# Two chained transformer blocks on one core: modulation weights regrouped by feature tile, the first projection woven between the modulation sums

## The reference

```python
silu_c = jax.nn.silu(c)
silu_cc = jax.nn.silu(c_ctx)
mod_l = (silu_c @ ada_w[l] + ada_b[l])[:, None, :]
mod_c = (silu_cc @ ada_w[l] + ada_b[l])[None, None, :]
sh1, sc1, g1, sh2, sc2, g2 = jnp.split(mod_l, 6, axis=-1)
csh1, csc1, cg1, csh2, csc2, cg2 = jnp.split(mod_c, 6, axis=-1)
hl = rms_norm(xl, norm_mix_w[l]) * (1 + sc1) + sh1
hc = rms_norm(xc, norm_mix_w[l]) * (1 + csc1) + csh1
pl = hl @ w_in
pc = hc @ w_in
```

## Time and profile before

| what | value |
|---|---|
| median of 3 runs | 2367.29 us |
| the runs | 2364.22 to 2369.87 us |
| profiled execution, first to last instruction | 2361.5 us (its time outside this span is not recorded) |
| mean granted TensorE clock | 0.983 |
| TensorE busy | 2267.3 us, 96% |
| TensorE weight load busy | 1935.6 us, 82% |
| VectorE, ScalarE, GpSimd busy | 50%, 36%, 40% |

### The profile page before, as it was taken

One profiled execution on the slowest core, in us unless ns is written; L12 is line 12 of the kernel. 1 busy time (PEld: TensorE's weight loads), 2 busy tenths in 40 slices (PEclk: granted clock), 3 DMA queues, 4 the chain that ended last, 5 costly groups with the idle time before them and its releaser, 6 DMA issues.

```text
span 2361.5 us, 37027 instructions
## 1 busy us (share of the span) xinstructions
PE 2267.3 (96%) x14111; PEld 1935.6 (82%) x14111; DVE 1179.9 (50%) x1904; ACT 860.2 (36%) x1411; POOL 939.8 (40%) x770
## 2 busy tenths in 40 slices
PE   6999999999999999999999999999999999999998
PEld 3878889888888888898888878778887887788776
DVE  4785763457777743343143365653333106671273
ACT  5434343241111122335315442223443236543462
POOL 2435442343343433334422255565665440254302
PEclk9999999999999999999999999999999999999998
DMA  7132232135555521112200025553222321122212
GB/s 282 63 144 72 99 126 68 63 125 187 187 186 194 187 99 62 63 62 72 60 14 10 28 92 185 182 193 104 95 92 96 98 89 64 57 81 89 68 46 72
DMA packets 66121, 245.42 MB, mean 104 GB/s; under 512 B 7312, under 2 KB 9616, under 8 KB 65360
## 3 DMA queue, kind: packets, MB, share of 16 engines
q1 hardware_dynamic: 65760, 242.94, 30.0%
q0 software_dynamic: 240, 0.79, 0.1%
HBM read 240.81 MB, written 2.10 MB: 103 GB/s over the span
## 4 chain that ended last, share of the span: by engine, by line
PE 68%; issue 6%; POOL 5%; DVE 4%; ACT 2%; POOLq 0%; DVEq 0%; ACTq 0%
PE ps L862 12%; PE ps L863 11%; PE ps L864 11%; POOL w_low L480 4%; PE ps L1663 4%; PE ps L1665 4%; PE ps L1666 4%; PE ps L1907 2%; PE ps L1894 2%; PE ps L623 2%; PE ps L1880 2%; PE ps L1832 1%; PE ps L899 1%; PE ps L900 1%; PE ps L901 1%
## 5 line engine op out<-in xcount | busy, mean ns | idle before, releaser
L480 POOL TENSOR_TENSOR w_low<-ring,w_high 128x512 fp32r<-128x512 f32 (+2 forms) x534 | 755.8, 1437 | 1126.9 <-ACT w_high L471 1113.9
L471 ACT ACTIVATE w_high<-ring 128x1024 fp32r<-128x1024 f32 (+2 forms) x267 | 274.7, 1031 | 951.4 <-PE ps L864 632.5
L862 PE MATMUL ps<-h_high,w_high 128*128 128x512 f32 x1040 | 412.8, 397 | 17.0 <-POOL h_low L725 7.1
L863 PE MATMUL ps<-h_low,w_high 128*128 128x512 f32 x1040 | 407.6, 392 | 0.0
L864 PE MATMUL ps<-h_high,w_low 128*128 128x512 f32 x1040 | 407.3, 392 | 0.0
L862 PEld LDWEIGHTS ps<-h_high,w_high 128*128 128x128 f32 x1040 | 196.7, 189 | 70.9 <-issue 14.0
L864 PEld LDWEIGHTS ps<-h_high,w_low 128*128 128x128 f32 x1040 | 196.5, 189 | 42.1
L863 PEld LDWEIGHTS ps<-h_low,w_high 128*128 128x128 f32 x1040 | 197.0, 189 | 37.7
L2977 DVE TENSOR_TENSOR hidden<-arena,hidden 128x1536 fp32r<-128x1536 f32 (+1 forms) x42 | 87.2, 2076 | 193.3 <-ACT hidden L2223 193.3
L1663 PE MATMUL ps<-hidden,w_high 128*128 128x512 f32 (+1 forms) x504 | 178.7, 355 | 0.0
L1665 PE MATMUL ps<-hidden,w_high 128*128 128x512 f32 (+1 forms) x504 | 178.6, 354 | 0.0
(11 more groups left out here) (488 smaller groups left out, 4816.1 us busy)
## 6 DMA issues: line engine op xcount, KB each, us to landing
const<-late_w_dram SPq DMA_DIRECT2D x112, 512.0 KB, 4.9
ring<-up_dram SPq DMA_DIRECT2D x88, 512.0 KB, 3.5
ring<-down_dram SPq DMA_DIRECT2D x44, 512.0 KB, 3.4
XB<-ada_dram SPq DMA_DIRECT2D x22, 768.0 KB, 5.4
ring<-winE_dram SPq DMA_DIRECT2D x32, 512.0 KB, 3.6
ring<-win_dram SPq DMA_DIRECT2D x20, 512.0 KB, 3.4
ring<-winC_dram SPq DMA_DIRECT2D x20, 512.0 KB, 3.6
arena<-ada_dram SPq DMA_DIRECT2D x10, 768.0 KB, 18.2
```

What stands on the lines that cost most here:

```text
L471: nc.scalar.activation(WH[p][:, 0:L], RAW[p][:, 0:L], ACT.Copy).then_inc(w_hi, 1)
L480: ins = nc.gpsimd.tensor_tensor(WL[p][:, to], RAW[p][:, to], WH[p][:, to].bitcast(F32), ALU.subtract)
L862: nc.tensor.matmul(bank[:, 0:n], wh[:, cols], hi, start=(k == 0), stop=False)
L863: nc.tensor.matmul(bank[:, 0:n], wh[:, cols], lo, start=False, stop=False)
```

## The change

The modulation weights are regrouped. `FIRST_TILES` lists six groups in which the shift and the scale of a feature tile come together: (8, 0, 9), (1, 10, 2), (11, 3, 12), (4, 13, 5), (14, 6, 15), (7). `first_columns(g)` takes the place of `mod_column` and `gains` for them: on VectorE, one add for each column tile, a wait for them, one small instruction for each gain, a wait again.

The norm's mean follows the first group's sums, the two segments share one mean sum and one root, and the latent spread comes before the second group's sums. Each feature tile of the latent segment is then scaled, shifted and split as soon as its group is there. `first_latent(k)` multiplies latent tile k by both of win0's first two chunks, six matmuls into two PSUM banks, and these calls stand between the sums and the turns of the groups. On ScalarE `shift_high` of the latent tiles is cut into pieces that stand between the calls of `mod_row`. The context segment follows after the latent one.

SP loads win0's chunks 0 and 1 behind the first group's weights instead of behind the last's. The copied rows of the first groups have a place of their own, and the banks of `adaT` and `n0` are changed.

```diff
--- before.py
+++ after.py
@@ -74,7 +74,9 @@
 
 
 
-MODS = [*range(0, 18, 3), *range(16, 46, 3), 45]
+FIRST_TILES = ((8, 0, 9), (1, 10, 2), (11, 3, 12), (4, 13, 5), (14, 6, 15), (7,))
+LATER_MODS = [*range(16, 46, 3), 45]
+MODS = [*FIRST_TILES, *LATER_MODS]
 ADA_COLS = 3 * P
 
 FIRST_MODS = 6
@@ -110,7 +112,7 @@
 )
 
 SUMS = dict(
-    adaT=(FIRST_MODS, (4, 5)), n0=(4, (0, 1, 2, 3)), win0=(19, B5), hgS0=(6 * SCORE_SUMS, (0, 1, 2, 3)), hgK0=(6 + ROUND_MODS[0], (5,)), hgU0=(12, (4, 6)), ro0=(5, (5, 6)),
+    adaT=(FIRST_MODS, (4,)), n0=(3, (1, 5, 6)), win0=(19, B5), hgS0=(6 * SCORE_SUMS, (0, 1, 2, 3)), hgK0=(6 + ROUND_MODS[0], (5,)), hgU0=(12, (4, 6)), ro0=(5, (5, 6)),
     win1=(19, B5), hgS1=(6 * SCORE_SUMS, (0, 1, 2, 3)), hgK1=(6 + ROUND_MODS[1], (5,)), hgU1=(12, (4, 6)), ro1=(5, (5, 6)),
     wmlp=(14, B5), sv=(8, B8), wout0=(16, B8),
     n1=(4, B8), up0=(88, B8), down0=(12, B8),
@@ -158,7 +160,7 @@
 
 PAIRED = (("n2", 0), ("n4", 0))
 
-BATCHED = dict(ro0=(range(4),), ro1=(range(4),), nlat=(range(1), range(1, 5)), nqk=(range(9), range(9, 21)), nB=(range(4),))
+BATCHED = dict(n0=(range(2),), ro0=(range(4),), ro1=(range(4),), nlat=(range(1), range(1, 5)), nqk=(range(9), range(9, 21)), nB=(range(4),))
 RS_COLS = 48
 PARTED = dict(n0=0, n1=2, n2=4, n3=6, n4=7, n5=8)
 
@@ -700,10 +702,10 @@
                 nc.scalar.wait_ge(h_even, KT // 2 * (PARTED[stage] + k) + j // 2 + 1)
                 nc.scalar.activation(dsts[j], dsts[j], ACT.Identity, bias=shifts[j]).then_inc(h_ready, 1)
 
-        def shift_high(stage, k, between=None):
+        def shift_high(stage, k, between=None, some=range(KT)):
 
             _, _, _, dsts, shifts, highs, _ = ITEMS[stage][k]
-            for j in range(KT):
+            for j in some:
                 if between and j == 4:
                     between()
                 await_scaled(nc.scalar, stage, k, j)
@@ -965,6 +967,7 @@
 
         ADA_EARLY, = carve((2 * FIRST_MODS, 4, ADA_COLS))
         ADA_ROW, = carve((3, ADA_COLS), at=ARENA - 3 * ADA_COLS)
+        ADA_ROW_EARLY, = carve((3, ADA_COLS), at=24 * T)
         ADA = [tiles(XB, 4 * ADA_COLS * c, 4, ADA_COLS) for c in range(ADA_SLOTS)]
         at = CONST_AT["masks"][0]
         LATE_W = [const[:, at + x * D:at + (x + 1) * D] for x in range(2)]
@@ -1009,6 +1012,9 @@
 
             return FIRST_MODS + sum(ROUND_MODS[:r]) + n
 
+        def ada_row_at(g):
+            return (ADA_ROW_EARLY if g < FIRST_MODS else ADA_ROW)[:, g % 3, :]
+
         def tiles_of(g):
             return 1 if g == FIRST_MODS - 1 else 3
 
@@ -1299,6 +1305,9 @@
             for u in range(2 * FIRST_MODS):
                 n = tiles_of(u // 2) * P
                 sp.dma_start(ADA_EARLY[:, u, :, 0:n], dram["ada"][u][:, :, 0:n]).then_inc(ada_early[u], 16)
+                if u == 1:
+                    for k in range(2):
+                        load_split(sp, "win0", k, k)
 
             def load_mods(chunks):
 
@@ -1308,8 +1317,6 @@
                         sp.wait_ge(ada_sums if half else ada_half, g + 1)
                     sp.dma_start(ADA[v % ADA_SLOTS], dram["ada"][2 * FIRST_MODS + v]).then_inc(ada_full[v % ADA_SLOTS], 16)
 
-            for k in range(2):
-                load_split(sp, "win0", k, k)
             sp.dma_start(const[:, tables_at:CONST_N], dram["const"][:, tables_at:]).then_inc(tables_in, 16)
             for k in range(2, 4):
                 load_split(sp, "win0", k, k)
@@ -1476,26 +1483,57 @@
                 bank = open_bank(pe, *turn_sums(g))
                 pe.wait_ge(ada_row, g + 1)
                 for i in range(tiles_of(g)):
-                    ins = nc.tensor.matmul(bank[:, 4 * i:4 * i + 4], ADA_ROW[:, g % 3, i * P:(i + 1) * P],
+                    ins = nc.tensor.matmul(bank[:, 4 * i:4 * i + 4], ada_row_at(g)[:, i * P:(i + 1) * P],
                                            C("pick")[:, 0:4], start=True, stop=True)
                 sums_done(ins, *turn_sums(g))
 
             pe.wait_ge(const_in, 32)
             pe.wait_ge(cs_ready, 3)
-            for g in range(FIRST_MODS):
-                mod_sums(g)
-                if g:
-                    mod_turn(g - 1)
-                for k in range(2):
-                    if g == 3:
-                        mean(pe, "n0", k)
-                    if g == 4:
-                        spread(pe, "n0", k)
-            mod_turn(FIRST_MODS - 1)
+
+            def first_latent(k):
+
+                h_there(pe, "n0")(0, k)
+                hi, lo = in_parts(0)(0, k)
+                cols = slice(k * P, (k + 1) * P)
+                for c in range(2):
+                    if k == 0:
+                        await_parts(pe, "win0", c)
+                        open_bank(pe, "win0", 2 * c)
+                    bank, p = bank_ap("win0", 2 * c), split_use("win0", c)[0]
+                    nc.tensor.matmul(bank, WH[p][:, cols], hi, start=(k == 0), stop=False)
+                    nc.tensor.matmul(bank, WH[p][:, cols], lo, start=False, stop=False)
+                    ins = nc.tensor.matmul(bank, WL[p][:, cols], hi, start=False, stop=(k == KT - 1))
+                    if k == KT - 1:
+                        sums_done(ins, "win0", 2 * c)
+
+            mod_sums(0)
+            for k in range(2):
+                mean(pe, "n0", k)
+            mod_turn(0)
+            spread(pe, "n0", 0)
+            mod_sums(1)
+            spread(pe, "n0", 1)
+            mod_turn(1)
+            first_latent(0)
+            mod_sums(2)
+            first_latent(1)
+            mod_turn(2)
+            first_latent(2)
+            mod_sums(3)
+            first_latent(3)
+            mod_turn(3)
+            mod_sums(4)
+            first_latent(4)
+            mod_turn(4)
+            first_latent(5)
+            mod_sums(5)
+            first_latent(6)
+            mod_turn(5)
+            first_latent(7)
 
             def first_chunks(x, stage):
 
-                for s in range(2):
+                for s in range(0 if x else 1, 2):
                     for c in range(2):
                         split_features(pe, stage, c, stage, 2 * c + s, KT, P, in_parts(x), (s,),
                                        ready=None if c else in_there(pe, x) if x else h_there(pe, "n0"))
@@ -2017,23 +2055,27 @@
             def mod_row(g):
                 act.wait_ge(ada_sums, g + 1)
                 cols = tiles_of(g) * P
-                A(ADA_ROW[:, g % 3, 0:cols], ps[:, ADA_BANK, 0:cols], ACT.Copy).then_inc(ada_row, 1)
+                A(ada_row_at(g)[:, 0:cols], ps[:, ADA_BANK, 0:cols], ACT.Copy).then_inc(ada_row, 1)
 
             act.wait_ge(x_in, 32)
             load_table(ROOT)
             for k, j in squared("n0"):
                 square("n0", k, j)
-                if k and j in (2, 4, 6):
-                    mod_row(j // 2 - 1)
-            mod_row(3)
-            for k in range(2):
-                root("n0", k)
-            mod_row(4)
-            mod_row(5)
+            mod_row(0)
+            root("n0", 0)
             for k in range(2):
                 split_hi("win0", k)
-            for k in range(2):
-                shift_high("n0", k)
+            mod_row(1)
+            shift_high("n0", 0, None, (0,))
+            mod_row(2)
+            shift_high("n0", 0, None, (1, 2))
+            mod_row(3)
+            shift_high("n0", 0, None, (3,))
+            mod_row(4)
+            shift_high("n0", 0, None, (4, 5))
+            mod_row(5)
+            shift_high("n0", 0, None, (6, 7))
+            shift_high("n0", 1)
 
             def y_high(y, to, n):
                 for k in range(KT):
@@ -2647,6 +2689,22 @@
             step.link(TT(small[:, 5:6], small[:, 4:5], small[:, 3:4], ALU.subtract))
             step.link(TS(small[:, 5:6], small[:, 5:6], -LAM_INIT, None, ALU.add))
 
+            def first_columns(g):
+
+                turned = await_sums(dve, *turn_sums(g))
+                for i, k in enumerate(FIRST_TILES[g]):
+                    ins = TT(mod[:, 0, k, :], turned[:, 4 * i:4 * i + 2], V("ab0", k).to_broadcast([P, 2]), ALU.add)
+                    if i < tiles_of(g) - 1:
+                        step.mark(ins)
+                taken(ins, *turn_sums(g))
+                step.settle()
+                await_taken(dve, *turn_sums(g))
+                for k in FIRST_TILES[g]:
+                    if k >= KT:
+                        step.mark(STT(gain[:, 0, k - KT, :], mod[:, 0, k, :], 1.0, V("nm0", k - KT).to_broadcast([P, 2]),
+                                      ALU.add, ALU.mult))
+                step.settle()
+
             def mod_column(g):
                 k, n = MODS[g], tiles_of(g)
                 turned = await_sums(dve, *turn_sums(g))[:, 0:4 * n].rearrange("p (i v) -> p i v", v=4)
@@ -2686,17 +2744,26 @@
             for k, j in squared("n0"):
                 if j:
                     add_square("n0", k, j)
-                if k and j in (4, 6):
-                    mod_column(j // 2 - 2)
-            for k in range(2):
-                invert("n0", k)
```

(33 more changed lines are left out.)

## The result

The kernel after takes 2381.56 us (median of 6 runs, 2380.67 to 2386.47) against 2366.75 us for the kernel before in the same set (6 runs, 2362.77 to 2369.87). The ratio is 1.0065, with a 95% interval of 1.0051 to 1.0080. It is slower by 14.8 us.

A forecast was written before the change was run, and what follows sets the result against it. TensorE was taken as the bound, so the start of win0's chunk 2 sets the time. Waits, products and sums at mostly low clock put it at 88.6, 24.3 us late: span 2385.8, time 2391.6, range 2377 to 2401.

The forecast's parts named there:

- the wide range: Whole kernel: time from 2377 to 2401 us, covering the forecast and both clock rivals' times with 3 us either side.
- High throughout: Rival for the start: waits of 2 to 3.9 us don't lower TensorE's clock; chunk 2 at 77.5, time 2380.5, chance 0.2.
- The start sets the rest: From win0's chunk 2 on TensorE is busy, so a microsecond won or lost there should reach the end.
- The queues: Feature loops: in-order TensorE and ScalarE make products wait on a three-engine chain, 3.2 us at tiles 1 and 3.
- The transfers cost nothing in this chain: Modulation weights: moved win0 loads delay transfers about 2.5 us each, free unless the chain is over a third shorter.
- The level of the clock: Feature loops: clock low again after each wait, rising after 5.7 us of unbroken work; chunk 2 at 88.6, 24.3 late.
- the prices: Start of the kernel: lengths per piece at two clock levels, such as latent products 2.6 us low or 1.4 high.
- Sums at the high level: Modulation sums on TensorE: one group's sums priced at 1.7 us at the high clock, 3.0 at the low.
- The 5.8 us outside the span: Whole kernel: the runs' median 2367.3 is 5.8 us above the 2361.5 span, and is added to the forecast span.

The follow-up runs named there:

- the kernel with the sums ahead: The kernel after, with each next group's sums ahead of the latent products and the last ScalarE row copy moved ahead of tile 5's shift; 2367.58 us, ratio 1.0004.
- the weights ahead: The kernel before, with win0's chunks 0 and 1 loaded behind the first group's modulation weights and rounded behind the roots; 2366.69 us, ratio 0.9997.
- filled waits: The kernel after, with unused idle matmuls put into TensorE's waits ahead of products 1, 3, 4, 6 and 7; 2379.32 us, ratio 1.0040.
- the products tile by tile: On top of the weights ahead, latent products of chunks 0 and 1 done tile by tile, not woven between the sums; 2365.12 us, ratio 0.9992.
- the split first: The kernel with the sums ahead, plus ScalarE rounding win0's chunk 2 ahead of the first three exponentials; 2363.45 us, ratio 0.9982.

## Why the prediction held, and where it was off

The time fell inside the wide range, and the mechanism, TensorE standing still behind three engines, was right. The value was not: half of the chance was on a chunk 2 that starts 24.3 us late, and it starts 13.9 late. What brought the time into the range was the room for the rival *High throughout*.

**The start sets the rest.** Right: 13.4 us at chunk 2 from the first sum, 13.9 on the axis of the span, 13.9 at the first scan, 14.0 at 872 us, and 14.8 between the medians.

**The queues.** Right, and shown by two edits of order, each on the kernel after: 7.7 us came back with ScalarE's, 14.6 with TensorE's (one row copy moved beside it). The sizes: forecast waits of 3.2, 3.2, 2.0, 1.9 and 3.9, measured 3.17, 3.17, 2.01, 1.79 and 3.80. Product 5's 1.14 was missing; at the low speed product 4 and the turn would have covered most of it.

**The transfers cost nothing in this chain.** Right in the kernel after. The step's condition, that they matter once the chain is more than a third shorter, was too cautious: in the kernel with the sums ahead the stretch from the second group's sums to product 7 is 24 us instead of 39, and no sums wait either. In the old order they do matter, 3.03 us.

**The level of the clock.** Wrong, and this is the step that failed: "After each wait I take the level as low again, as in 40 to 45 us". With it I put chunk 2 at 88.6, 24.3 late. The level fell after two of the six waits (3.17 at 44.6 and 3.80 at 64.1), each time for 3.4 us, and did not fall after a wait of 3.17 at 36.3 nor after the shorter ones. The rival *High throughout* had 77.5 for chunk 2 and 2380.5 for the time; measured 78.20 and 2381.56. I had taken the wrong row for a pattern: in 40 to 50 us of the kernel before, TensorE had stood still for 3.58 us and again, after one product, for 2.34. With the weights ahead only the first of these waits is there (3.68), and the low level lasts 3.4 us instead of 10. That fits the kernel after, where TensorE had a stretch of work between any two waits; why the level falls behind one wait and not behind another stays open.

The page of the Trainium skill that I weighed (TensorE: Matmul & The Clock Gate, section on HAM oscillation) tells of waits of about 3 to 5 us, each followed by a slow burst. Three waits here are that long: products 3 and 7 (3.17 and 3.80) are slow bursts behind them, product 1 (3.17) isn't. The shorter waits ahead of products 4, 5 and 6 are not the page's case, and I should not have put every burst under it.

**The rival's number is partly luck.** *High throughout* says that such waits don't lower the level; behind two of them it fell. Its 68.5 for the end of product 7 doesn't follow from the prices either: added up at the high level from 29 us on they give about 65.8, and chunk 2 at about 75. The missing 2.7 us are about what the low level cost at product 3 (1.6) and product 5's wait (1.14). A smaller slip of the same kind is in the forecast, where a run of 7.0 us with 5.7 at the low level saves 0.65 us and not 0.9.

**Sums at the high level** cost 1.50 a group, not 1.7: each half of 0.85 ends with a matmul of 0.50, which the next half overlaps when the two run on. This makes up for a part of what the sum lacked.

**The 5.8 us outside the span.** Wrongly named, and harmless. The executions of this study have 1.7 to 3.2 us between span and time (2378.6 and 2381.16 for the profiled one of the kernel after). So the profiled execution of the kernel before was probably about 3 us below its median. The time isn't touched by it: to add 24.3 to the span and then 5.8 is to add 24.3 to the median.

## What to carry to other kernels

Before work is woven between stages of another engine, write down for each pair of neighbours in a queue whether the second needs something that starts only when the first has ended; each such pair shows the whole chain as a wait, here 3.2 us over ScalarE and GpSimd. Put a stage of lead between them. Here it was enough to do that on TensorE, the engine that stood still: with the next group's sums ahead of the products all of the delay and 1.3 us more came back (14.6 us), and with ScalarE's order alone about half (7.7). The two don't add up. And look again at the next release after a gain: here the time saved went into a wait for a weight chunk, behind three exponentials and a slower low part on GpSimd, until the rounding was moved too.

## What the hardware showed that I had not expected

Waits of about 3 us move the granted clock one time and not another. After 3.17 us of standing still it stayed high in one place and fell in another place of the same execution; after 2.69 us ahead of chunk 2 it fell in two kernels (sums ahead, filled waits), after 1.33 and 0.94 it did not. In these cases TensorE was already at work again when it fell: product 3 starts at 47.76 and the level falls at about 47.9, product 7 at 67.95 and 68.4, chunk 2 of the kernel with the sums ahead at 63.95 and 65.3. A fall lasted 3.4 us each time at these places and cost about 1.7 us where TensorE was the bound. With the products tile by tile it fell without any such wait, while TensorE worked on the modulations' small matmuls, and stayed low for 13.6 us (0.26 x 4 x 2 = 2.1 in 34 to 38, then up to 49.5). So I take it that the same program can gain or lose some microseconds between executions, which is the size of what the smaller edits here bring; with one trace of each kernel no run shows that directly.

GpSimd and VectorE got in each other's way at chunk 2. Its low part is two instructions. With the sums ahead and with the filled waits VectorE's first instruction on the gates starts just as the first of the two ends (61.82 and 75.27 us); VectorE's takes 0.96 us and GpSimd's second 2.06 instead of 1.27. In the kernel after, VectorE's starts half a microsecond into GpSimd's second (77.43); GpSimd's takes 1.27 and VectorE's 1.54 instead of 0.96. With the split first they don't meet, and take 1.27 and 0.96. So the one that comes second is the slower. No run was made to test this, but it is the 0.8 us by which chunk 2 comes later than ScalarE would let it in the first two kernels.
